# RWKV chunk stage: a loop of two-turn steps written out as eight turns over which three turns' work is interleaved

## What is computed

```python
def step(S, inp):
    r_t, w_t, k_t, v_t, kk_t, a_t = inp
    sa = jnp.einsum('bhvk,bhk->bhv', S, -kk_t)
    S = (S * w_t[:, :, None, :] + sa[..., None] * (kk_t * a_t)[:, :, None, :]
         + v_t[..., None] * k_t[:, :, None, :])
    return S, jnp.einsum('bhvk,bhk->bhv', S, r_t)
xs = tuple(jnp.moveaxis(t, 1, 0) for t in (r, w, k, v, kk, a))
_, y = lax.scan(step, jnp.zeros((b, h, n, n), jnp.float32), xs)
```

## Time and profile before

| | us |
|---|---|
| median of three runs | 3068.24 |
| lowest, highest | 3062.13, 3073.23 |
| profiled execution, its own time | 3072.92 |
| its span in the profile | 3071.1 |
| chunk stage in it, first staging copy to last copy of y | 354.6 to 695.2 |
| mean granted clock of TensorE | 0.922 of full |

### The profile page before, as it was taken

The page is one execution under the profiler, slowest core; times in us unless marked ns, Lnnn a source line. Parts: engine busy times, 40 slices in busy tenths (PEclk is TensorE's granted clock), DMA queues, the critical chain, the costliest instruction groups (busy, mean ns, idle before and its releaser), DMA issues. The chain is left out here.

```text
span 3071.1 us, 53711 instructions
## 1 busy us (share of the span) xinstructions
PE 2634.0 (86%) x18332; PEld 2189.2 (71%) x18332; DVE 1945.2 (63%) x2179; ACT 1602.8 (52%) x1920; POOL 380.2 (12%) x342
## 2 busy tenths in 40 slices
PE   5997787885698999999927999999669799999991
PEld 4775677772575888888726888888657588888880
DVE  3358244344337899989753666656533798999884
ACT  3655122221224788788623555454421487888871
POOL 0020000000000333333201000000000022323220
PEclk8998898897898999999958999999779899999995
DMA  3110000000425999999641101000042599999974
GB/s 96 42 42 28 15 3 3 3 3 12 151 96 209 379 379 386 384 380 376 263 176 48 28 28 34 27 27 28 1 160 96 180 379 378 377 382 387 385 288 177
DMA packets 219958, 524.84 MB, mean 171 GB/s; under 512 B 43824, under 2 KB 99120, under 8 KB 219824
## 3 DMA queue, kind: packets, MB, share of 16 engines
q1 hardware_dynamic: 201392, 489.34, 43.1%
q0 software_dynamic: 18432, 33.60, 2.9%
HBM read 506.06 MB, written 50.33 MB: 181 GB/s over the span
## 5 line engine op out<-in xcount | busy, mean ns | idle before, releaser
L1604 DVE TENSOR_TENSOR w_low<-w_raw,w_high 128x1024 fp32r<-128x1024 f32 x768 | 894.2, 1218 | 29.8 <-DVEq L52 20.6
L1322 ACT CAST w_high<-w_raw 128x1024 fp32r<-128x1024 f32 x768 | 755.1, 1049 | 107.8 <-ACTq L52 107.7
L1470 PE MATMUL ps<-w_high,x_high 128*128 128x512 f32 x1024 | 414.6, 405 | 6.8 <-PEq L52 6.2
L1474 PE MATMUL ps<-w_high,x_low 128*128 128x512 f32 x1024 | 403.4, 394 | 0.0
L1473 PE MATMUL ps<-w_low,x_high 128*128 128x512 f32 x1024 | 401.6, 392 | 0.0
L1470 PEld LDWEIGHTS ps<-w_high,x_high 128*128 128x128 f32 x1024 | 195.2, 191 | 49.5 <-issue 13.0
L1865 PE MATMUL ps<-h_high,w_high 128*128 128x512 f32 x512 | 212.5, 415 | 16.2 <-PEq L52 16.2
L1474 PEld LDWEIGHTS ps<-w_high,x_low 128*128 128x128 f32 x1024 | 194.0, 189 | 43.1
L1473 PEld LDWEIGHTS ps<-w_low,x_high 128*128 128x128 f32 x1024 | 195.0, 190 | 37.4
L1470 PE MATMUL ps<-w_high,hidden_high 128*128 128x512 f32 x512 | 200.9, 392 | 6.7 <-PEq L52 6.7
L1865 PE MATMUL ps<-h_high,w_low 128*128 128x512 f32 x512 | 202.1, 395 | 0.0
(11 more groups left out here) (407 smaller groups left out, 5086.1 us busy)
## 6 DMA issues: line engine op xcount, KB each, us to landing
w_raw<-in_moe_w_gate SPq DMA_DIRECT2D x256, 512.0 KB, 5.4
w_raw<-in_moe_w_up SPq DMA_DIRECT2D x256, 512.0 KB, 5.7
w_raw<-in_moe_w_down SPq DMA_DIRECT2D x256, 512.0 KB, 5.6
w_raw<-expert_rows SPq DMA_DIRECT2D x32, 512.0 KB, 10.8
w_tiles<-in_c_w_in SPq DMA_DIRECT2D x32, 512.0 KB, 4.0
w_tiles<-in_ab_w_in SPq DMA_DIRECT2D x22, 512.0 KB, 3.9
residual<-in_x SPq DMA_DIRECT2D x16, 512.0 KB, 8.8
h_rows<-hn_moe SPq DMA_DIRECT2D x16, 512.0 KB, 2.9
```

The costliest lines, as they stand in the source:

```text
L1322: act.copy(wh[:, p, :], raw[:, p, :]).then_inc(high_made, 1)
L1470: ins = pe.matmul(ps[:, bank, :], high, w_h, start=first, stop=False)
L1474: return pe.matmul(ps[:, bank, :], low, w_h, start=False, stop=final)
L1604: dve.tensor_tensor(wl[:, p, :], raw[:, p, :], wh[:, p, :].bitcast(F32), ALU.subtract).then_inc(low_made, 1)
```

## The change

`rwkv_chunks` is written anew; nothing outside it changes. It computes the same products with the same masks.

- The staging tiles and their copies are gone: TensorE reads `ab`, `bb`, `r`, `k`, `v` in place. Grams of 64x128 become two of 64x64.
- The loop is gone: Python writes out all eight turns, with waits on absolute counts.
- The grams are copied from PSUM by ScalarE (`gram_out`, `low_copy`, `gram_k_out`) and VectorE masks them from SBUF. `LO` gets its own tile in place of free columns of `proj`. tok and XT exist three times, X twice.
- T1's two groups share a PSUM bank and are copied by one copy of 512 columns.
- Turn f's levels are the frame. Between T1 and dx of a level, and behind dx, stand parts of turn f+1's rows and grams and of turn f-1's sequence. `ds_y` is split in `ds` and `y_rows`.
- VectorE makes the level's masks one at a time between the levels' additions, and within `x_add` XT's addition no longer waits for X's.

The core of the diff (new side; the old side is printed above; indentation cut):

```diff
+        tok = sb("row_major", [P, 3, 3, NI, HD])
+        XT, X = sb("x_inv_t", [P, 3, NI, HD]), sb("x_inv", [P, 2, NI, HD])
+        LO, T1 = sb("low_levels", [P, NLV, NI, HD]), sb("t1", [P, NI, HD])
+        MK, RB = sb("masked_k", [P, 2, 2, NI, HD]), sb("masked_rb", [P, 2, NI, HD])
+        LT, LW, MT = sb("gram_b", [P, 2, NI, 2, HD]), sb("gram_low", [P, NI, HD]), sb("gram_k", [P, 2, NI, 2, HD])
...
+        gram = rows_of(ps[:, 0:2, :])
+        low = ps[:, 2, :].rearrange("p (i n) -> p i n", n=HD)
...
+        ROWS = ((k, 2, 2), (v, 0, 0), (bb, 1, 1))
+        t1_at = lambda g: ps[:, 3, g * W:(g + 1) * W]
+        dx_at = lambda g, m: ps[:, 4 + g, m * W:(m + 1) * W]
...
+        def rows(f, m):
+            src, bk, _ = ROWS[m]
+            if f:
+                pe.wait_ge(low_out if m == 0 else mt_out, f)
+            for n in range(NI):
+                ci, j = divmod(n, NPAIR)
+                for h, q in halves:
+                    last = pe.matmul(ps[q, bk, js(n)], src[q, j, chunk(f, ci)], eye[h], start=True, stop=True)
+            last.then_inc(rows_done, 1)
+        def gram_b(f, ci):
+            pe.wait_ge(tok_ready, 3 * f + 2 + ci)
+            tk = chunk(f, ci)
+            for j in range(NPAIR):
+                n = ci * NPAIR + j
+                for mv, to in ((ab, gram[:, n, 0, :]), (r, gram[:, n, 1, :])):
+                    for h, q in halves:
+                        pe.matmul(to[q], bb[q, j, tk], mv[q, j, tk], start=True, stop=True)
+                for h, q in halves:
+                    last = pe.matmul(low[q, n], ab[q, j, tk], bb[q, j, tk], start=True, stop=True)
+            last.then_inc(lt_done, 1)
+        def gram_k(f):
+            pe.wait_ge(lt_out, 2 * f + 2)
...
+        def t1(f, lv):
+            pe.wait_ge(lo_done, NLV * f + lv + 1)
+            if lv == 0:
+                pe.wait_ge(x_first, f + 1)
+            for g in range(2):
+                if lv:
+                    pe.wait_ge(x_next, 2 * (NLV * f + lv) - 1 + g)
+                for j in range(NPAIR):
+                    for h, q in halves:
+                        n = g * NPAIR + j
+                        last = pe.matmul(t1_at(g)[q, js(j)], LO[q, lv, n, :], X[q, f % 2, n, :], start=True, stop=True)
+            last.then_inc(t1_done, 1)
+        def dx(f, lv):
+            pe.wait_ge(t1_copied, NLV * f + lv + 1)
...
+        def u(f, ci):
+            pe.wait_ge(s_ready, 2 * f + ci + 1)
+            pe.wait_ge(mk_done, f + 1)
...
+        def sa(f, ci):
+            pe.wait_ge(u_copied, 2 * f + ci + 1)
+            pe.wait_ge(x_next, 2 * NLV * (f + 1) - 1 + ci)
+            if f or ci:
+                pe.wait_ge(y_copied, 2 * f + ci)
...
+        for m in range(3):
+            rows(0, m)
+        gram_b(0, 0)
+        gram_b(0, 1)
+        gram_k(0)
+        for f in range(NTURN):
+            nxt, seq = f + 1 < NTURN, f > 0
+            t1(f, 0)
+            if seq:
+                u(f - 1, 0)
+            if nxt:
+                rows(f + 1, 0)
+            dx(f, 0)
+            if nxt:
+                rows(f + 1, 1)
+                rows(f + 1, 2)
+            t1(f, 1)
+            if seq:
+                sa(f - 1, 0)
+            dx(f, 1)
+            if nxt:
+                gram_b(f + 1, 0)
+            t1(f, 2)
+            if seq:
+                ds(f - 1, 0)
+            dx(f, 2)
+            if nxt:
+                gram_b(f + 1, 1)
+            t1(f, 3)
+            if seq:
+                u(f - 1, 1)
+            dx(f, 3)
+            if seq:
+                y_rows(f - 1, 0)
+            t1(f, 4)
+            if seq:
+                sa(f - 1, 1)
+            if nxt:
+                gram_k(f + 1)
+            dx(f, 4)
+            if seq:
+                ds(f - 1, 1)
+                y_rows(f - 1, 1)
+        f = NTURN - 1
+        for ci in range(2):
+            u(f, ci)
+            sa(f, ci)
+            if ci == 0:
+                ds(f, ci)
+            y_rows(f, ci)
...
+        def gram_out(f, ci):
+            act.wait_ge(lt_done, 2 * f + ci + 1)
+            if f >= 2:
+                act.wait_ge(masks_done, f - 1)
+            act.copy(LT[:, f % 2, ci * NPAIR:(ci + 1) * NPAIR].rearrange("p i m n -> p (i m n)"), ps[:, ci, :]).then_inc(lt_out, 1)
...
+        def t1_out(f, lv):
+            act.wait_ge(t1_done, NLV * f + lv + 1)
+            act.copy(T1[:].rearrange("p i n -> p (i n)"), ps[:, 3, :]).then_inc(t1_copied, 1)
...
+        for f in range(NTURN):
+            nxt, seq = f + 1 < NTURN, f > 0
+            t1_out(f, 0)
             if seq:
+                u_out(f - 1, 0)
+            if nxt:
+                tok_out(f + 1, 0)
+                tok_out(f + 1, 1)
+            t1_out(f, 1)
+            if nxt:
+                tok_out(f + 1, 2)
             if seq:
+                sa_out(f - 1, 0)
+            t1_out(f, 2)
+            if nxt:
+                gram_out(f + 1, 0)
+            t1_out(f, 3)
+            if nxt:
+                low_copy(f + 1)
             if seq:
+                u_out(f - 1, 1)
+            if nxt:
+                gram_out(f + 1, 1)
             if seq:
+                y_out(f - 1, 0)
+            t1_out(f, 4)
             if seq:
+                sa_out(f - 1, 1)
+            if nxt:
+                gram_k_out(f + 1)
             if seq:
+                y_out(f - 1, 1)
...
+        def x_start(f):
+            dve.wait_ge(low_out, f + 1)
+            ch(dve.tensor_tensor(X[:, f % 2], LW[:], bcast(c.lower_1, 1, NI), ALU.mult))
+            dve.tensor_tensor(X[:, f % 2], X[:, f % 2], bcast(ident64, 1, NI), ALU.add).then_inc(x_first, 1)
+        def xt_start(f):
+            dve.wait_ge(lt_out, 2 * f + 2)
+            ch(dve.tensor_tensor(XT[:, f % 3], LT[:, f % 2, :, 0, :], up(0), ALU.mult))
+            dve.tensor_tensor(XT[:, f % 3], XT[:, f % 3], bcast(ident64, 1, NI), ALU.add)
+        def level(f, lv):
+            dve.tensor_tensor(LO[:, lv], LT[:, f % 2, :, 0, :], up(lv + 1), ALU.mult).then_inc(lo_done, 1)
+        def masks_r(f):
+            dve.tensor_tensor(RB[:, f % 2], LT[:, f % 2, :, 1, :], bcast(c.strict_incl[:, 1, :], 1, NI), ALU.mult).then_inc(masks_done, 1)
+            dve.wait_ge(mt_out, f + 1)
             for m in range(2):
+                ins = dve.tensor_tensor(MK[:, f % 2, m], MT[:, f % 2, :, m, :], bcast(c.strict_incl[:, m, :], 1, NI), ALU.mult)
+            ins.then_inc(mk_done, 1)
...
+        dve.memset(SS[:, 0], 0.0).then_inc(s_ready, 1)
+        x_start(0)
+        xt_start(0)
+        level(0, 0)
+        for f in range(NTURN):
+            nxt, seq = f + 1 < NTURN, f > 0
+            level(f, 1)
+            x_add(f, 0)
+            level(f, 2)
+            level(f, 3)
+            x_add(f, 1)
+            level(f, 4)
+            if seq:
+                state(f - 1, 0)
+            x_add(f, 2)
+            masks_r(f)
+            x_add(f, 3)
+            if nxt:
+                x_start(f + 1)
+            x_add(f, 4)
+            if nxt:
+                xt_start(f + 1)
+                level(f + 1, 0)
+            if seq:
+                state(f - 1, 1)
+        state(NTURN - 1, 0)
```

More of the change, by code:

```diff
@@ L729, in _ @@
             @block.scalar
             def _(act):
[L731 to L735, removed]
-                    pairs = [(ab, AR[:, f, :, :, 0, :]), (r, AR[:, f, :, :, 1, :]), (bb, BS), (k, KS), (v, VS)]
-                    copies = [(src, dst, ci) for src, dst in pairs for ci in range(2)]
-                    for src, dst, ci in copies[part::3]:
-                        link(act.copy(dst[:, ci], src[:, :, bass.ds(turn * P + ci * HD, HD)]))
-                    if part == 2:
-                        act.sem_inc(s["staged"], 1)
@@ L744, in rows_out @@
-                def rows_out(f):
-                    take(act, s["turned_done"])
-                    for m in range(3):
-                        link(act.copy(tok[:, f, m].rearrange("p i n -> p (i n)"), ps[:, B_TOK[m], :]))
-                    act.sem_inc(s["tok_ready"], 1)
-                def t1_out():
-                    for g in range(2):
-                        take(act, s["t1_done"])
-                        act.copy(chunk_items(T1, g).rearrange("p i n -> p (i n)"), ps[:, B_T1[g], 0:W]).then_inc(s["t1_copied"], 1)
@@ L914, in _ @@
-                step(0, seq=False)
-                with pe.Fori(0, NTURN // 2 - 1):
-                    step(1)
-                    step(0)
-                step(1)
-                step(0, front=False)
+                        y_out(f - 1, 1)
+                f = NTURN - 1
+                for ci in range(2):
+                    u_out(f, ci)
+                    sa_out(f, ci)
+                    y_out(f, ci)
             @block.vector
             def _(dve):
-                def link(ins):
-                    ins.then_inc(s["order"], 1)
-                    take(dve, s["order"])
+                ch = Chain(dve, order)
@@ L956, in state @@
-                def state(turn, ci):
-                    take(dve, s["ds_done"])
```

(18 more changed lines are left out.)

278 lines of the change are left out of this document (91 added, 187 removed).

## The result

The changed kernel takes 2982.2 us (median of 4 runs, 2982.0 to 2986.5), the kernel before 3065.2 (4 runs, 3061.6 to 3073.2): ratio 0.9733, 95% interval 0.9716 to 0.9749. That is 83 us less; forecast were 80, and 2988 us. Between the two profiled executions it is 90.9 (3072.9 and 2982.0).

A forecast was written before the change was run, and what follows sets the result against it. TensorE was nearest to a bound, but some 14 us of a 42.3 us turn were chain waits and low clock. The stage gains 87.8 us less 8 for instruction fetch, 80: 3068.2 to 2988 us, range 2974 to 3014.

The forecast's parts named there:

- Part 1: Work per turn in the chunk stage: nothing computed less; TensorE 960 narrow records, 28.1 us; VectorE about 17, ScalarE near 10.
- Part 2: Waits between T1 and dx in each level: fillers cover most, 0.57, 0.1, 0.1 and 0.6 us open; steady turn 29.5 us.
- Part 3: Start, first and last turns and closing sequence: T1 starts at 367.8 us, stage ends at 607.4, 87.8 us earlier.
- Part 4: Instruction fetch in TensorE's dense stretches: stands cost 1 us a turn, 8 us in the stage, taken off the gain.
- Rival (a): Instruction fetch in the stage: it hides fully, no stand at all; gain 88 us, 2980 us; chance 0.11.
- The sum: Whole stage: 87.8 us gained less 8 for the instruction stream, 80 us, giving a median of 2988 us.
- (b): Instruction fetch binds: a 0.7 us stand at each packet, turns of 34 to 35 us, 3022 us; chance 0.17.
- (c): TensorE's clock falls as before: some 3 us a turn, 24 us, time 3012 us; chance 0.12.
- (d): TensorE is granted its lower clock level through the whole stage: slower, 3205 us; chance 0.03.
- (e): VectorE's in-order queue holds back what TensorE's fillers uncover: no wait goes, the time stays; chance 0.02.

The follow-up runs named there:

- better order: Changed kernel with the rows' third part moved behind level 1's T1 and, on VectorE, the next turn's first low triangle ahead of the fifth addition; 2975.4 us.

## Why the prediction was right

The range 2974 to 3014 holds the time, and the forecast's mechanism is in the trace. Point by point:

- **Part 1, the work.** Right. 960 records in a turn, 29.3 ns apart when read in place: 28.2 us for turn 1 of the better order is the bound of 28.1 itself. VectorE (15.9) and ScalarE (9) stay under TensorE.
- **Part 2, the waits of a level.** Right in place, twice too large in size. Forecast 0.57 at sa in level 1, 0.1 in levels 2 and 3, 0.6 at the border; the starts of after show 0.40, nothing, nothing and 0.30. A steady turn is 29.0 and not 29.5. The hand-offs were taken from rows of before, where each wait drags a decrement behind it. With such instructions put back on all engines the new kernel's starts show 0.57 at sa, 0.10 in levels 2 and 3, and 0.4 to 0.7 at the border, close to the forecast. (The distance of starts, less the 0.03 of a record, is 0.19 more than the idle time in a row's brackets, which counts from the modelled end.) So the walk was correct for a kernel that the change does not leave standing: the diff's new form of the waits was listed and not priced.
- **Part 3, the ends.** From TensorE's start to T1 12.2 us (forecast 13.2), turn 0 26.7 (27.6), turns 1 to 6 175.4 (177), turn 7 and the tail 33.9 (35.0). The stand of 3 us at the end of turn 0 was 2.5, and the clock fell behind it, 1.5 us that turn 1 had not been given. In all 235.9 us from T1 of turn 0 to the last copy, against 239.6.
- **Part 4, the instruction stream.** Wrong in size: 8 us were taken off and no such stand is in the stage of after. The stand of 0.68 us at 438.40 most likely does belong to the fetch, as the prediction had it, since it ends 1.3 us after a packet has landed. The step that failed is the inference that it carries over to the new code, at 1 us a turn. In the old kernel with the decrements gone, at the same 960 records in a turn, such stands are gone; in the new kernel with semaphore instructions added they return. Rival (a), no stand at all, was right on this term. After passes a packet each 29.0 x 127.5 / 960 = 3.85 us, by estimate, without a stand. The Trainium skill ("Runtime: NRT & Kernel Launch", section "Instruction fetch mechanics") says that crossing a block is mostly hidden, and after agrees. The better order does not: with no wait left, there is a stand of 0.1 to 0.5 us at most packets.
- **The sum.** From profile to profile the stage gave 92.5 us where the walk had 87.8 and the forecast 80, so 12.5 more. Between the medians the gain is 83, only 3 more: the rest of the program took 1.7 longer, and the profiled execution of before lay 7.7 us above its median (four runs; 4.7 by the three runs of the forecast), while that of after lies on its median. Outside the stage the execution of before took 2730.5 us, which is ordinary among the kernels, so part of the 7.7 may lie in the stage, whose usual length would then be under 340.6. The other 3 us of the miss are the median of before, 3065.2 now and 3068.2 then. So the number is closer than its terms, and that is luck: stands that did not come and a profiled execution above the median cancel.
- **Rivals (b) to (e).** (b) fell for this order; turns of 34 us do not occur, though the better order sees its beginning. (c) held for one turn of eight, at 1.5 us; its 24 us for a clock that falls as before are near the 29 that the clock gave back by the estimate above. (d) and (e) did not happen: the clock is 1.00 in seven of eight turns, VectorE is waited for only at the border.

What stays open: why the instructions come late where TensorE's stream holds semaphore instructions. That the stands are the fetch itself rests on their distance from the packets' landing; no run changed the fetch alone. Nor is it told why the same stand of 2.35 us lowers the clock at some times and not at others.

## What to carry to other kernels

Give each engine a row for what it issues without a record in the profile: a semaphore instruction behind each wait cost 62 ns on average on a TensorE that is nearly dense, with some 30 of them in a turn of 29 us, and in the chained order the 401 of the other two engines cost 18.4 us. Waits on absolute counts, which a written-out loop makes possible, were worth 16 to 29 us here, next to 35 to 47 for the rest of the rewrite. When filling a chain, give each wait filler longer than the whole hand-off, and place another engine's next-turn work ahead of its last addition of this turn. Once no wait is left, the stream of small instructions can be what bounds, as in three turns here. A stand with no releaser is worth holding against the landing of the instruction packets.

## What was not expected of the hardware

- TensorE's clock stayed at 1.00 through turns with ten stands of 0.3 to 1.1 us each, and fell to a mean of 0.67 to 0.71 over the next 5 to 6 us behind four of six equal stands of 2.35 us.
- Stands of TensorE with no releaser ended 1.2 to 1.6 us after an instruction packet of 16 KB had landed, in 39 of 40 rows. One packet each 3.85 us passed without a stand; where the records would use one up in 3.74 us, they came each 3.97 and most brought a stand of 0.1 to 0.5 us.
- Such stands, of up to 1.5 us in the old kernel written out and in place, were gone when only the form of TensorE's waits changed.
